# A gated recurrence in a two-layer decoder step: one block, state increments first, samples' states scaled on ScalarE

## The reference, cut to what matters

```
S_t = diag(f_t) S_{t-1} + k_t v_t^T          o_t = S_t^T q_t
f = lb + (1 - lb) * sigmoid(z)               k = (1 - lb) * sigmoid(-z)

chunk of the prompt:
  o_inter = einsum('bhtk,bhkv->bhtv', qc * exp(b), S)
  attn    = einsum('bhtk,bhtsk,bhsk->bhts', qc, decay, kc)
  o_intra = einsum('bhts,bhsv->bhtv', attn, vc)
  S_new   = exp(b_last) * S + einsum('bhsk,bhsv->bhkv', kc * exp(b_last - b), vc)
each sample: one such step from its own stored state (8 states of 4 x 128 x 128)
```

## Time and profile before

| | |
|---|---|
| time, median of 3 runs | 4379.13 us (4376.19 to 4380.94) |
| profiled execution, its own time | 4380.36 us |
| profiled execution, span | 4378.6 us |
| PE busy | 4121.6 us (94%) |
| PEld busy | 3707.9 us (85%) |
| DVE busy | 2531.3 us (58%) |
| ACT busy | 1181.0 us (27%) |
| POOL busy | 38.3 us (1%) |

### The profile page before, as it was taken

How to read it: one execution, slowest core, us unless ns; L and a number is a source line. 1 busy time by engine, 2 the same in 40 slices (tenths; PEclk the granted TensorE clock), 3 DMA queues, 4 the chain that set the end, 5 groups by cost and what they waited for, 6 DMA issues and landing times. The chain is left out here.

```text
span 4378.6 us, 74431 instructions
## 1 busy us (share of the span) xinstructions
PE 4121.6 (94%) x27209; PEld 3707.9 (85%) x27209; DVE 2531.3 (58%) x4688; ACT 1181.0 (27%) x1587; POOL 38.3 (1%) x43
## 2 busy tenths in 40 slices
PE   8777779999999999999998988999999999999997
PEld 8754479999999998888887567999999998888886
DVE  3642247777776535555554755777777534555555
ACT  2101042233333321111113443333333332111112
POOL 0000000000000010000000000000000001000000
PEclk9869789999999999999999988999999999999999
DMA  3026523334444565555541012233454466555562
GB/s 108 24 77 208 185 77 105 111 129 173 155 170 169 178 236 197 187 197 189 198 146 67 29 39 96 102 124 135 167 185 154 166 207 221 198 187 199 184 201 82
DMA packets 321924, 652.36 MB, mean 149 GB/s; under 512 B 26241, under 2 KB 157442, under 8 KB 321154
## 3 DMA queue, kind: packets, MB, share of 16 engines
q1 hardware_dynamic: 318978, 642.36, 43.1%
q0 software_dynamic: 2816, 8.40, 0.5%
HBM read 509.00 MB, written 141.53 MB: 149 GB/s over the span
## 5 line engine op out<-in xcount | busy, mean ns | idle before, releaser
L1797 DVE TENSOR_TENSOR experts_ul<-experts_u,experts_uh 128x1024 fp32r<-128x1024 f32 x512 | 627.1, 1225 | 1068.5 <-ACT experts_uh L1691 1062.2
L1584 PE MATMUL ps<-peer_x_then_r_xh,experts_ul 128*128 128x260 f32 x4096 | 1166.4, 285 | 0.0
L1585 PE MATMUL ps<-experts_over_x_xl,experts_uh 128*128 128x260 f32 x4096 | 1154.9, 282 | 0.0
L1586 PE MATMUL ps<-peer_x_then_r_xh,experts_uh 128*128 128x260 f32 x4096 | 1153.6, 282 | 0.0
L1691 ACT ACTIVATE experts_uh<-experts_u 128x1024 fp32r<-128x1024 f32 x512 | 540.6, 1056 | 1094.6 <-PE ps L1648 1085.2
L1646 PE MATMUL ps<-experts_over_a_ah,experts_ul 128*128 128x512 f32 x2048 | 796.9, 389 | 0.0
L1648 PE MATMUL ps<-experts_over_a_ah,experts_uh 128*128 128x512 f32 x2048 | 796.9, 389 | 0.0
L1647 PE MATMUL ps<-experts_over_a_al,experts_uh 128*128 128x512 f32 x2048 | 796.8, 389 | 0.0
L1584 PEld LDWEIGHTS ps<-peer_x_then_r_xh,experts_ul 128*128 128x128 f32 x4096 | 771.7, 188 | 0.0
L1586 PEld LDWEIGHTS ps<-peer_x_then_r_xh,experts_uh 128*128 128x128 f32 x4096 | 770.1, 188 | 0.0
L1585 PEld LDWEIGHTS ps<-experts_over_x_xl,experts_uh 128*128 128x128 f32 x4096 | 769.8, 188 | 0.0
(11 more groups left out here) (347 smaller groups left out, 4681.7 us busy)
## 6 DMA issues: line engine op xcount, KB each, us to landing
experts_u<-peer_u SPq DMA_DIRECT2D x256, 512.0 KB, 3.3
experts_u<-peer_v SPq DMA_DIRECT2D x256, 512.0 KB, 3.3
hidden<-experts_act SPq DMA_DIRECT2D x256, 260.0 KB, 2.2
gates<-experts_over_b_g SPq DMA_DIRECT2D x128, 512.0 KB, 3.0
experts_over_b_g<-gates SPq DMA_DIRECT2D x128, 512.0 KB, 4.9
experts_act<-hidden SPq DMA_DIRECT2D x256, 256.0 KB, 3.6
mla_ct<-cache SPq DMA_DIRECT2D x64, 320.0 KB, 3.8
pa_ct<-cache SPq DMA_DIRECT2D x64, 320.0 KB, 3.7
```

The lines of the kernel that those rows point to most:

```text
L1584: pe.matmul(o, ul[:, b % 4, c], xh[:, c, h, 0:TH], start=(c == 0), stop=False)
L1585: pe.matmul(o, uh[:, b % 4, c], xl[:, c, h, 0:TH], start=False, stop=False)
L1586: mm = pe.matmul(o, uh[:, b % 4, c], xh[:, c, h, 0:TH], start=False, stop=(c == KC - 1))
L1797: v.tensor_tensor(ul[:, b % 4], u[:, b % 2], uh[:, b % 4].bitcast(F32), ALU.subtract).then_inc(split_done, 1)
```

## The change

The three blocks become one.

- `turn_values` goes. PE transposes the sample rows first, then the 16 prompt tiles, then spreads all eight rows of `vs` into eight PSUM banks. ACT copies them to a new tile `spread`, two banks at a time.
- SP loads all eight sample states at the start into `one`, instead of two and then one by one. ACT scales them in place by `f` (now `fs`, 8 columns per head), one head of one sample at a time.
- DVE no longer copies `kd` and `pre` for level 0 and no longer forms `kd` for level 1, and ACT no longer copies `q`: PE reads `kk` and `q` directly. POOL clears five tiles instead of two.
- Levels 0 to 4 are taken into `attn` by DVE as before, levels 5 to 7 by ACT as rectangular copies.
- A sample's step on DVE is four fused instructions (one per head). Three samples are done before the turned keys are copied, one after, four at the end.
- The turned keys are copied half by DVE, half by ACT, into the memory of `suf`. PE computes all four state increments first, DVE forms four states from them with fused instructions per head, then PE computes the outputs, with the samples' read-outs among them; ACT copies the outputs to `cat`.

The core of the diff (the removed second block and other removed lines are in the kernel above):

```diff
-def turn_values(nc, k, proj, vt, vs):
...
+    ON_ACT = 5
...
+        spread = s.sb("spread", [P, TS, H, P])
+        one = s.sb("one", [P, TS, H, P])
+        states = s.sb("states", [P, NCH, H, P])
+        kt = suf[:].rearrange("p h (c d) -> p h c d", c=NCH)
...
                 sp.dma_start(masks[:], a["masks"]).then_inc(landed, 16)
+                for n in range(TS):
+                    sp.dma_start(one[:, n], a["state_hgrn"][n]).then_inc(one_landed, 16)
+                for n in range(TS):
+                    sp.wait_ge(new_ready, n + 1)
+                    sp.dma_start(a["new_hgrn_s"][n], one[:, n]).then_inc(stored, 16)
+                    if n == TS // 2:
+                        sp.wait_ge(state_ready, NCH)
+                        sp.dma_start(a["new_hgrn_p"], states[:, NCH - 1]).then_inc(stored, 16)
+                sp.wait_ge(stored, 16 * TS + 16)
+
+            @block.gpsimd
+            def _(pool):
+                pool.memset(attn[:], 0.0).then_inc(cleared, 1)
+                pool.memset(suf[:], 1.0).then_inc(cleared, 1)
+                pool.memset(kd[:, 0], 0.0).then_inc(cleared, 1)
+                pool.memset(qd[:, 0], 0.0).then_inc(cleared, 1)
+                pool.memset(kd[:, 1], 0.0).then_inc(cleared, 1)
 
             @block.scalar
             def _(act):
                 act.wait_ge(lb_m, 1)
                 act.activation(lb[:, 0:3], lb[:, 0:3], ACT.Exp).then_inc(lb_e, 1)
-                act.activation(f[:], proj[:, H:2 * H], ACT.Sigmoid).then_inc(sig, 1)
+                act.activation(pre[:], proj[:, H:2 * H, 0:TP], ACT.Sigmoid)
+                act.activation(fs[:], proj[:, H:2 * H, TP:T], ACT.Sigmoid).then_inc(sig, 1)
                 act.activation(kk[:], proj[:, H:2 * H], ACT.Sigmoid, scale=-1.0).then_inc(sig, 1)
-                act.activation(qd[:, 0], q[:, :, 0:TP], ACT.Copy).then_inc(q_copied, 1)
+                for n in range(0, TS, 2):
+                    act.wait_ge(v_spread, n + 2)
+                    act.activation(spread[:, n:n + 2].rearrange("p n h d -> p n (h d)"), k.ps[:, n:n + 2, :], ACT.Copy
+                                   ).then_inc(spread_read, 1)
                 act.activation(gate, gate, ACT.Silu)
+                act.wait_ge(fs_ready, 1)
+                act.wait_ge(one_landed, 16 * TS)
+                for n in range(TS):
+                    for h in range(H):
+                        ins = act.activation(one[:, n, h], one[:, n, h], ACT.Copy, scale=fs[:, h, n:n + 1])
+                    ins.then_inc(scaled, 1)
+                act.wait_ge(level_read, ON_ACT)
+                for level in range(ON_ACT, LEVELS):
+                    m = 1 << (level - 1)
+                    act.wait_ge(level_ready, level + 1)
+                    bank = 4 * (level % 2)
+                    for b in range(0, CL, 2 * m):
+                        rows, cols = slice(b, b + m), slice(b + m, b + 2 * m)
+                        new = k.ps[rows, bank:bank + 4, :].rearrange("s h (c t) -> s (h c) t", t=CL)
+                        ins = act.activation(attn[rows].rearrange("s h c t -> s (h c) t")[:, :, cols], new[:, :, cols], ACT.Copy)
+                    ins.then_inc(act_read, 1)
+                act.wait_ge(turned, 2)
+                act.activation(kt[:, 2:4].rearrange("s h c d -> s h (c d)"), k.ps[:, 2:4, :], ACT.Copy).then_inc(kt_act, 1)
+                for c in range(NCH):
+                    act.wait_ge(chunk_ready, c + 1)
+                    act.activation(cat[:, 0:H, c * CL:(c + 1) * CL], k.ps[:, 4 + c, :].rearrange("p (h t) -> p h t", h=H), ACT.Copy)
...
+                v.wait_ge(v_turned, 1)
+                v.tensor_copy(vs[:], k.ps[0:TS, 0, :]).then_inc(v_copied, 1)
...
+                v.wait_ge(v_turned, 2)
+                v.tensor_copy(vt[:], k.ps[:, 4:4 + NCH, :]).then_inc(v_copied, 1)
 
                 v.wait_ge(sig, 1)
                 for h in range(H):
+                    v.tensor_scalar(pre[:, h], pre[:, h], lb[:, 5, h:h + 1], lb[:, 4, h:h + 1], ALU.mult, ALU.add)
                 v.wait_ge(sig, 2)
                 for h in range(H):
                     ins = v.tensor_scalar(kk[:, h], kk[:, h], lb[:, 5, h:h + 1], None, ALU.mult)
-                chain(ins)
-                v.tensor_copy(kd[:, 0], kk[:, :, 0:TP]).then_inc(decayed, 1)
-                chain(v.tensor_copy(pre[:], f[:, :, 0:TP]))
-                v.wait_ge(cleared, 2)
-                v.wait_ge(landed, 16)
+                ins.then_inc(decayed, 1)
+                chain(v.tensor_tensor(fs[:], fs[:], bc(lb[:, 5], 2, TS), ALU.mult))
+                v.tensor_tensor(fs[:], fs[:], bc(lb[:, 4], 2, TS), ALU.add).then_inc(fs_ready, 1)
...
+                    if level > 1:
+                        v.tensor_tensor(kdv[:, :, :, ks], kkv[:, :, :, ks], sv[:, :, :, ks], ALU.mult)
                     v.tensor_tensor(qdv[:, :, :, qs], qv[:, :, :, qs], pv[:, :, :, qs], ALU.mult).then_inc(decayed, 1)
-                    take(level - 1)
+                    if level == 1:
+                        v.wait_ge(cleared, 1)
+                        v.wait_ge(landed, 16)
+                    if level - 1 < ON_ACT:
+                        take(level - 1)
+
+                def sample(n):
+                    v.wait_ge(spread_read, TS // 2)
+                    v.wait_ge(scaled, n + 1)
+                    for h in range(H):
+                        ins = v.scalar_tensor_tensor(one[:, n, h], spread[:, n, h], kk[:, h, TP + n:TP + n + 1], one[:, n, h],
+                                                     ALU.mult, ALU.add)
+                    ins.then_inc(new_ready, 1)
+
+                for n in range(3):
+                    sample(n)
                 v.wait_ge(turned, 1)
-                v.tensor_copy(kt[:].rearrange("s h c d -> s (h c d)"), k.ps[:, 0:4, :].rearrange("s b d -> s (b d)")
-                              ).then_inc(kt_ready, 1)
+                v.tensor_copy(kt[:, 0:2].rearrange("s h c d -> s h (c d)"), k.ps[:, 0:2, :]).then_inc(kt_dve, 1)
+                sample(3)
                 for c in range(NCH):
+                    v.wait_ge(inc_ready, c + 1)
+                    new = k.ps[:, c, :].rearrange("p (h d) -> p h d", h=H)
                     if c == 0:
-                        v.tensor_copy(state[:], new).then_inc(chunk_read, 1)
+                        v.tensor_copy(states[:, 0], new).then_inc(state_ready, 1)
                     else:
+                        v.wait_ge(state_ready, c)
+                        last = pre[:].rearrange("p h (c t) -> p h c t", t=CL)
+                        for h in range(H):
+                            ins = v.scalar_tensor_tensor(states[:, c, h], states[:, c - 1, h], last[:, h, c, CL - 1:CL], new[:, h],
+                                                         ALU.mult, ALU.add)
+                        ins.then_inc(state_ready, 1)
+                for n in range(4, TS):
+                    sample(n)
+                v.wait_ge(read_out, TS)
+                v.tensor_copy(cat[:, 0:H, TP:T], k.ps[:, 0, 0:TS * H].rearrange("p (n h) -> p h n", h=H))
 
             @block.tensor
...
+                for h in range(H):
+                    mm = pe.transpose(k.ps[0:TS, 0, h * P:(h + 1) * P], proj[:, MIX - H + h, TP:T], k.ident[:])
+                mm.then_inc(v_turned, 1)
+                for c in range(NCH):
+                    for h in range(H):
+                        mm = pe.transpose(k.ps[:, 4 + c, h * P:(h + 1) * P], proj[:, MIX - H + h, c * CL:(c + 1) * CL], k.ident[:])
+                mm.then_inc(v_turned, 1)
+                for n in range(TS):
+
+                    if n == 0:
+                        pe.wait_ge(v_copied, 1)
+                    if n == 4:
+                        pe.wait_ge(v_copied, 2)
+                    pe.matmul(k.ps[:, n, :], k.ident[0:TS, n:n + 1].broadcast_to([TS, P]), vs[:], start=True, stop=True
+                              ).then_inc(v_spread, 1)
+
                 for level in range(LEVELS):
                     pe.wait_ge(decayed, level + 1)
-                    pe.wait_ge(q_copied, 1)
-                    if level >= 2:
+                    if level < 2:
+                        pe.wait_ge(spread_read, TS // 4 * (level + 1))
+                    elif level - 2 < ON_ACT:
                         pe.wait_ge(level_read, level - 1)
+                    else:
+                        pe.wait_ge(act_read, level - 1 - ON_ACT)
                     for h in range(H):
                         for c in range(NCH):
                             t = slice(c * CL, (c + 1) * CL)
-                            mm = pe.matmul(k.ps[:, 4 * (level % 2) + h, t], kd[:, level % 2, h, t], qd[:, level % 2, h, t],
-                                           start=True, stop=True)
+                            ks = kk[:, h, t] if level < 2 else kd[:, level % 2, h, t]
+                            qs = q[:, h, t] if level < 1 else qd[:, level % 2, h, t]
...
                 pe.wait_ge(decayed, LEVELS + 1)
```

(44 more changed lines are left out.)

120 lines of the change are left out of this document (19 added, 101 removed).

## The result

The changed kernel takes 4335.66 us (median of 4 runs, 4330.28 to 4338.36) against 4377.79 us of the kernel before (median of 4 on the same chip): 42.1 us less, ratio 0.990 with a 95% interval of 0.9888 to 0.9911. The forecast was 4338 in 4326 to 4352. The profiled execution is the fastest of the four, 4330.28 us with a span of 4328.5 us, 50.1 us under the span before. Both numbers are right; why they differ is the first question of the experiments.

The account below looks back on a forecast made before the run. It took DVE to bound the levels, PE the samples, and both by turns the chunks. Front +1, levels -2.4 and tail -39.5 gave -41 us, so 4338 us, range 4326 to 4352.

Parts of the forecast that it names:

- middle price of the clock: Tail: PE passes priced between warm 0.11 and cold 0.213 us, at 0.16 for increments and outputs, 0.153 for read-outs.
- the forecast's own case: Whole kernel: the main outcome, a gain of 34 to 48 us, given chance 0.60.
- Front: Stretch up to level 0's `take`: savings and added work about cancel, ending 1 us later than before.
- I take 156.1: Front: DVE's 4-column instruction waits for all five POOL memsets and ends at 156.1, not at 149.7 without waiting.
- 166 to 170 as the sign: Front: level 0's `take` was to start at 166 to 170 us if the forecast held.
- if it ends at 149.7, the front is 5 us better: Front: if DVE's 4-column instruction does not wait for POOL's memsets, the front gains 5 us.
- Levels: DVE-bound level loop: `take` of levels 5 and 6 leaves DVE's path, 1.20 us each, -2.4 us.
- Tail: From level 8's end to the next stage: 4.55 us, then 23.9 of PE work, then 1.5, about 30; -39.5 us.
- rival 3: Small DVE instructions cost 1.88 us each instead of 0.27: 84 us more, time 4422; chance 0.02 with everything slower.
- rival 1: Front early with `take(0)` at 162.5, PE warm throughout, tail 22.8 us: -53.6 us, time 4325.5; chance 0.16.
- what was named as wrong: Tail: forecast wrong if turned keys' copy to next stage takes under 20 or over 37 us.
- Rival 2: PE cold throughout, `take(0)` at 172.8, tail 38.5 us: -27.6 us, time 4351.5; chance 0.20.

Follow-up runs that it names:

- after_again: The changed kernel with no edit, run and profiled a second time: median 4335.62 us, block 94.1 us, tail 28.9 us.
- late_clear: Changed kernel, but POOL clears the three tiles the change added only after the keys are scaled: block 92.6 us, front 18.5 us.
- takes_on_dve: Changed kernel, but DVE instead of ACT takes levels 5 to 7 into `attn`: levels 47.4 us, block 96.2 us.
- samples_apart: Changed kernel, but the samples again have their own block with two buffers, loads one by one and full-width operations: tail 47.4 us, block 111.4 us.
- apart_serial: Changed kernel, but samples in their own block and each state increment behind its chunk's output: tail 54.6 us, block 118.3 us.
- level0_first: Changed kernel, but PE does spreads 4 to 7 between levels 0 and 1: front 18.5 us, levels 49.2 us, block 95.4 us.
- best: Changed kernel with read-outs mixed among output products, POOL clearing after scaled keys, turned values copied earlier, two spreads behind level 0: median 4331.0 us.
- reads_last: Changed kernel, but all 64 read-out passes stand behind the last chunk in PE's queue: median 4336.64 us, tail 28.9 us.

## Why the prediction was right, point by point

**The whole.** -41 us was forecast on the profiled execution, which gave -50.1; the medians differ by 42.1. The forecast took its tail at a middle price of the clock. The common case, as after_again shows, is a block of 94.1 us and so -42.4, near the forecast; the profiled case is 88.0 and -48.5, and its -50.1 lies outside the -34 to -48 of the forecast's own case.

**Front: +1 forecast, -1.2 in the profile and +0.3 in after_again.** The size held within 2.2 us and the reasoning behind it was half wrong. The step "I take 156.1", that L519 sits through all five memsets, failed: it waited for one, and ended at 150.3. What the step missed is that the four scalings of `pre` would then meet the next memsets: 2.5 us there (late_clear). The keys were scaled at 158.5 and not at 162.0. The spreads had no pause in the middle, ended at 159.4 and fell to the lower clock while PE was full. A spread was priced at 2.07 us, from a row of one standing alone; in a row, the spreads' weight loads follow one another by 0.43 us at the higher level and 0.85 at the lower, two to a spread, so 1.71 us at most. Both errors made the forecast late: `take(0)` at 165.2 against 168 forecast and 166 to 170 as the sign, in a block that started 0.6 us earlier. That the miss is no larger is luck, since level 0 ran close to its cold price, 5.67 us against 5.9. The sign "if it ends at 149.7, the front is 5 us better" failed as well: L519 was nearly that early, and PE held the front. "The front part gives nothing back" stands within those 1.2 us.

**Levels: -2.4 forecast, -2.1 measured.** The DVE-bound loop behaved as its rows said, and takes_on_dve confirms it. The loads and ACT's 32 scalings cost nothing: the scalings took 9.45 us from 163.70 to 173.1, twenty-three us before level 5's copy at 196.6, where 175 was forecast as their end.

**Tail: T + 30 forecast (T is the end of level 8's products), 24.3 and 28.9 measured.** The fused instruction's price was right: 12 in 3.23 us, 0.27 us each, and rival 3, small instructions at the price of L489, is excluded. The increments began at T + 4.4, 4.55 forecast. From there the PE work was 18.5 us in the profile, up to 233.4, where 23.9 was forecast; in after_again it was about 23.3 (217.06 to 240.33). By terms, 14.1 us were forecast for the 88 passes of increments and outputs and 9.8 for the read-outs; they took 11.4 and 7.1 us in the profile, 14.0 and 9.3 in after_again. So the middle price fits the common case, and the profile is the warm case of rival 1. The price of 0.16 was called the chunks' mean, but the clock of 0.67 in the earlier trace rows is a mean that includes idle time, and the same row's busy time, 20.47 us for 104 passes, gives 0.20 a pass, or 17.3 us for 88. That the chunks would run faster than before had no reason in the working; here the forecast was lucky. From the end of the turned keys' copy to the next stage it took 20.0 us in the profile, on the edge of what was named as wrong, and 24.6 in after_again. DVE ended at 226.2, PE alone bounded, as forecast.

**Rivals.** The profiled run came 3.5 us short of rival 1 (-53.6), whose second half, PE at the higher level in the whole tail after the increments' middle, is what it shows; the first, an early front, did not come. Rival 2, cold throughout, did not come in any profile of the merged block. Its reason did in part: the clock fell in the spreads, and in after_again in the read-outs.

**Where the gain came from.** The forecast named 6.5 us for the start of the samples' block and left the rest undivided. samples_apart and apart_serial divide it as 14.9, 7.2 and 18.5 us, single profiles each. The 6.5 us stand in the trace of before as the 6.64 us of DVE ahead of its first sample's step; no experiment removed them alone. What the forecast did not name is the clock, 7.0 of the 14.9 us.

## What to carry to other kernels

When small dependent blocks on different engines follow one another, merging them so that one engine's leftovers fill another's waits was worth more here (18.5 us) than the reordering inside one of them (7.2 us). Before costing either, look whether TensorE stands at the lower clock, since the same passes cost 0.11 or 0.21 us; 7.0 us of this gain are that. Spread one-column matmuls among dense ones instead of bunching them; for the passes over 8 rows, putting some of them behind level 0 (level0_first, best) brought no gain. A single profile of such a block can be 6 us off its common case, so take a second one before explaining a difference of that size.

## What the runs showed of the hardware

- The granted clock fell with PE busy in every microsecond: in a row of 512-column passes over 8 rows of contraction (6.40 of 6.40 us at 0.50), towards the end of 32 one-column passes (0.92, then 0.50 in after_again), and within 64 of them (5.00 of 5.00 us at 0.50 in reads_last). In the first profile the same two rows of 32 stayed at 1.00, 3.63 us each. With four one-column passes at a time between dense ones it stayed at 1.00 for 13.3 us.
- A DVE `tensor_scalar` and a POOL memset wait for one another: 4 columns took 1.51 us beside memsets and 0.17 without, four of 512 columns 4.45 us and 1.91. A DVE copy from PSUM (2.29 us) and a product of two SBUF tensors (2.28 us) were not slowed by the same memsets. The four of `pre` took 1.53, 2.10, 0.53 and 0.53 us: the first ended 0.28 us after the fourth memset, the second 0.27 us after the fifth, and the fifth memset, between them, took 2.08 us instead of 1.80.
